# Causal mask and cumulated forget logarithms of the attention: from float32 matmuls to single-pass (float32r) matmuls, the logarithms as high and low parts

## The reference

```python
s = einsum('bqhd,bkhd->bhqk', q[:, q0:q1], k[:, :q1]) * scale
if cum is not None:
    s = s + (cq - ck)                 # cum = cumsum(log_sigmoid(f_logit + b))
s = where((k_pos <= q_pos) & key_valid, s, NEG_INF)
p = softmax(s); out = einsum('bhqk,bkhd->bqhd', p, v[:, :q1])
...
o_mla = block_causal_attention(q, k, v, 96 ** -0.5, key_valid)          # 8 heads
o_fox = block_causal_attention(fq, fk, fv, 64 ** -0.5, key_valid, cum)  # 8 heads
```

## Time and profile before

| | us |
|---|---|
| median of 3 runs | 1728.81 |
| those runs | 1722.48 to 1732.06 |
| profiled execution, its own time | 1722.41 |
| its span, first to last instruction | 1720.6 |
| PE busy (89% of the span) | 1523.9 |
| DVE busy (60%) | 1026.8 |
| MLA half of the attention, about | 342 to 370.5 |
| fox half of the attention, about | 370.5 to 415 |
| output projection, about | 415 to 445 |

### The profile page before, as it was taken

One profiled execution on the slowest core, in us unless ns is written; L12 is line 12 of the kernel. 1 busy time (PEld: TensorE's weight loads), 2 busy tenths in 40 slices (PEclk: granted clock), 3 DMA queues, 4 the chain that ended last, 5 costly groups with the idle time before them and its releaser, 6 DMA issues.

```text
span 1720.6 us, 22658 instructions
## 1 busy us (share of the span) xinstructions
PE 1523.9 (89%) x8228; PEld 1161.9 (68%) x8228; DVE 1026.8 (60%) x2104; ACT 533.0 (31%) x1069; POOL 558.6 (32%) x361
## 2 busy tenths in 40 slices
PE   6999989999699999999999989878787778777876
PEld 6999988678599999998889988433333333333332
DVE  5554355655233325998984744657676766758555
ACT  4443353352244335443116421312121212121111
POOL 3555353000134432001001402454454544444540
PEclk9999999899799998999999999898999998899998
DMA  6666699819979997998975836799999999999994
GB/s 264 241 227 247 245 350 378 279 46 342 386 284 371 370 366 284 365 371 308 346 255 196 342 105 275 307 428 426 428 426 427 427 427 427 426 427 427 427 427 194
DMA packets 98724, 571.87 MB, mean 332 GB/s; under 512 B 10960, under 2 KB 11088, under 8 KB 48976
## 3 DMA queue, kind: packets, MB, share of 16 engines
q1 hardware_dynamic: 60624, 297.89, 47.3%
q0 software_dynamic: 36864, 268.45, 37.1%
q10 hardware_dynamic: 1152, 4.43, 0.7%
HBM read 569.68 MB, written 135.27 MB: 410 GB/s over the span
## 4 chain that ended last, share of the span: by engine, by line
PE 67%; DMA 20%; DVE 8%; issue 2%; ACT 2%; SPq 2%; POOL 0%; ACTq 0%; DVEq 0%; POOLq 0%
DMA arena<-pairs,eidx 16%; PE ps L2125 11%; PE ps L1612 9%; PE ps L1614 9%; PE ps L1613 9%; PE ps L1957 5%; PE ps L2090 3%; PE ps L1663 2%; PE ps L1665 2%; PE ps L1664 2%; DMA ring<-pairs,eidx 2%; PE ps L1974 2%; DVE arena L1530 2%; DMA ring<-in_stream 1%; PE ps L1627 1%
## 5 line engine op out<-in xcount | busy, mean ns | idle before, releaser
L2125 PE MATMUL ps<-arena 128*128 128x512 f32 x720 | 346.3, 636 | 85.3 <-ACT arena L997 85.2
L634 POOL TENSOR_TENSOR w_lo<-ring,w_hi 128x1024 fp32r<-128x1024 f32 x82 | 216.2, 2638 | 446.7 <-DVE w_lo L1059 366.3
L2125 PEld LDWEIGHTS ps<-arena 128*128 128x128 f32 x720 | 144.2, 204 | 285.5 <-issue 174.1
L1612 PE MATMUL ps<-u_hi,w_hi 128*128 128x256 f32 (+1 forms) x1056 | 305.1, 289 | 9.9 <-DVE u_lo L1028 9.9
L1614 PE MATMUL ps<-u_hi,w_lo 128*128 128x256 f32 (+1 forms) x1056 | 303.3, 287 | 0.0
L1613 PE MATMUL ps<-u_lo,w_hi 128*128 128x256 f32 (+1 forms) x1056 | 302.9, 287 | 0.0
L1530 DVE CUSTOM_DVE_ANT_0 arena<-arena 128x1024 f32<-128x1024 f32 x180 | 218.9, 1223 | 138.7 <-DMA arena<-pairs,eidx 138.7
L664 POOL DMA_INDIRECT arena<-pairs,eidx x180 | 213.4, 1185 | 254.8 <-PE ps L2125 202.4
L681 ACT ACTIVATE w_hi<-ring 128x1024 fp32r<-128x1024 f32 x188 | 197.9, 1056 | 191.5 <-PE ps L1665 77.5
L1612 PEld LDWEIGHTS ps<-u_hi,w_hi 128*128 128x128 f32 x1056 | 201.9, 191 | 12.6 <-issue 10.7
L1614 PEld LDWEIGHTS ps<-u_hi,w_lo 128*128 128x128 f32 x1056 | 202.2, 192 | 0.0
(11 more groups left out here) (301 smaller groups left out, 2461.0 us busy)
## 6 DMA issues: line engine op xcount, KB each, us to landing
ring<-in_stream SPq DMA_DIRECT2D x130, 1024.0 KB, 7.0
pairs<-in_peer_u SPq DMA_DIRECT2D x128, 512.0 KB, 7.6
pairs<-in_peer_v SPq DMA_DIRECT2D x128, 512.0 KB, 8.8
arena<-in_ada SPq DMA_DIRECT2D x32, 768.0 KB, 6.3
arena<-pairs,eidx POOLq DMA_INDIRECT x180, 17.9
ring<-pairs,eidx POOLq DMA_INDIRECT x76, 17.3
h<-in_x_t SPq DMA_DIRECT2D x1, 1088.0 KB, 7.8
arena<-in_keys ACTq DMA_DIRECT2D x1, 1024.0 KB, 7.0
```

The source lines that it names most:

```text
L634: pool.tensor_tensor(lo[:, half, :], ring[:, slot, e * HALF:(e + 1) * HALF], hi[:, half, :], ALU.subtract).then_inc(used if e else lo_done, 1)
L1612: pe.matmul(dst, hi[:, half, block], x[0][:, b, 0:w], start=(b == 0), stop=False)
L2125: mm = pe.matmul(ps[:, Y_BANKS[j // TOPK] + half, :], diag[:, n % DIAGS, :], slot_of(n)[:, D + half * 512:D + half * 512 + 512], start=(hd ...
```

## The change

The mask and the identity are copied once by ScalarE into float32r tables (`masking`), the column table `sel` with sign plus and minus into `signs`. VectorE makes, instead of `ncumz`, a float32r copy of `cumz` (`cum_hi`) and the remainder (`cum_lo`). TensorE adds the mask with one float32r matmul, and the logarithms with four (high and low, along queries and along keys) instead of two float32 ones; the minus sign moves into the `signs` table.

```diff
-        ncumz = view(T)
+        place(parts_end)
+        cum_hi, cum_hi_f = parts("cum_hi", 1, T)
+        cum_lo, _ = parts("cum_lo", 1, T)
+        masking, _ = parts("masking", 2, P)
+        signs, _ = parts("signs", 2, HEADS)
...
# ScalarE, between the raw queries and the raw keys
+            act.activation(masking[:, 0, :], ident, ACT.Copy).then_inc(masking_made, 1)
+            act.activation(masking[:, 1, :], C("neg_mask"), ACT.Copy).then_inc(masking_made, 1)
+            act.activation(signs[:, 0, :], C("sel"), ACT.Copy).then_inc(masking_made, 1)
+            act.activation(signs[:, 1, :], C("sel"), ACT.Copy, scale=-1.0).then_inc(masking_made, 1)
...
# VectorE, before the first maximum
-            dve.tensor_scalar(ncumz, cumz, -1.0, None, ALU.mult).then_inc(cum_done, 1)
+            dve.wait_ge(q_raw_mm, 4)
+            then(dve.tensor_copy(cum_hi[:, 0, :], cumz), cum_done)
+            dve.tensor_tensor(cum_lo[:, 0, :], cumz, cum_hi_f[:, 0, :], ALU.subtract).then_inc(cum_done, 1)
...
# TensorE, scores_of(n)
-                    pe.matmul(dst, cumz[:, X0 + t * P:X0 + (t + 1) * P], C("sel")[:, f:f + 1].broadcast_to([P, keys_n]), start=False, stop=False)
-                    pe.matmul(dst, C("sel")[:, f:f + 1].broadcast_to([P, P]), ncumz[:, 0:keys_n], start=False, stop=False)
-                pe.matmul(ps[:, n % 3, keys_n - P:keys_n], ident, C("neg_mask"), start=False, stop=True).then_inc(s_mm, 1)
+                    for cum in (cum_hi, cum_lo):
+                        pe.matmul(dst, cum[:, 0, X0 + t * P:X0 + (t + 1) * P], signs[:, 0, f:f + 1].broadcast_to([P, keys_n]),
+                                  start=False, stop=False)
+                        pe.matmul(dst, signs[:, 1, f:f + 1].broadcast_to([P, P]), cum[:, 0, 0:keys_n], start=False, stop=False)
+                if n == 0:
+                    pe.wait_ge(masking_made, 4)
+                pe.matmul(ps[:, n % 3, keys_n - P:keys_n], masking[:, 0, :], masking[:, 1, :], start=False, stop=True).then_inc(s_mm, 1)
```

More of the change, by code:

```diff
@@ L269, in program @@
         assert spot[0] <= act_end - RING * T
+        place(parts_end)
[3 more added lines that the diff above has]
+        signs, _ = parts("signs", 2, HEADS)
+        assert spot[0] <= parts_end + 2 * HEADS * QK
         place(split)
@@ L427, in program @@
         cum_done = sem("cum_done")
+        masking_made = sem("masking_made")
         kpe_done = sem("kpe_done")
@@ L1856, in scores_of @@
                     if f + t == 0:
-                        pe.wait_ge(cum_done, 3)
+                        pe.wait_ge(cum_done, 4)
                     pe.matmul(dst, fqz[:, f, q], fk[:, f // 2, 0:keys_n], start=True, stop=False)
-                    pe.matmul(dst, cumz[:, X0 + t * P:X0 + (t + 1) * P], C("sel")[:, f:f + 1].broadcast_to([P, keys_n]), start=False, stop=False)
-                    pe.matmul(dst, C("sel")[:, f:f + 1].broadcast_to([P, P]), ncumz[:, 0:keys_n], start=False, stop=False)
-                pe.matmul(ps[:, n % 3, keys_n - P:keys_n], ident, C("neg_mask"), start=False, stop=True).then_inc(s_mm, 1)
+                    for cum in (cum_hi, cum_lo):
[5 more added lines that the diff above has]
+                pe.matmul(ps[:, n % 3, keys_n - P:keys_n], masking[:, 0, :], masking[:, 1, :], start=False, stop=True).then_inc(s_mm, 1)
             def turn_probs(n):
```

## The result

| | before | changed |
|---|---|---|
| median, us | 1728.01 (8 runs, 1721.44 to 1732.06) | 1742.06 (8 runs, 1735.08 to 1745.95) |
| profiled execution, its own time | 1722.41 | 1735.38 |
| mean granted clock of that execution | 0.950 | 0.935 |

The ratio is 1.0081, 95% interval 1.0056 to 1.0106: slower by less than 1% but clear of the scatter, where 1726.9 us (range 1719.5 to 1733) and no measurable change were forecast. In a second measurement of the changed kernel it was 1.0115 [1.0051, 1.0178]. The profiled executions differ by 12.97 us.

A forecast was written before the change was run, and what follows sets the result against it. The DMA queue, not TensorE, was taken to set the second feed-forward's start. Terms -0.8 - 0.28 - 0.6 + 0.45 - 0.7 gave -1.9 us, from 1728.81 to 1726.9 us, range 1719.5 to 1733.

The forecast's parts named there:

- the clock falls: Rival: lighter streaming drops TensorE's clock in the MLA half, +3.1 us a pair, some +25 us, 1752 us; chance 0.04.
- T0: SyncE's issue at 379.92 us after the first modulation addition; savings before it count, later ones mostly lengthen TensorE's 15.58 us idle.
- Prices of the single-pass matmuls: Attention on TensorE: a float32r matmul costs 0.124 us over 272 columns, 0.11 over 144 or 128.
- Single-pass is not single-pass: Rival: broadcast operands make the float32r logarithm matmuls cost float32's price; 1738.3 us; chance 0.03.
- MLA pair: Two MLA attention units, 3.91 us: lighter odd mask saves 0.13 us per loop, about six loops, -0.8 us.
- Fox pair: Two fox attention units, 4.99 us: TensorE saves 0.70, taken as -0.6 us, one full pair before T0.
- VectorE ahead of the first maximum: Before the first softmax: copy and subtraction replace the negation, so the first maximum starts 0.45 us later.
- ScalarE's four copies: Between raw queries and raw keys: about 0.9 us, covered by ScalarE's waits for TensorE, cost 0; uncovered up to 1.5.
- After T0: Fox half: TensorE's some 3 us saved goes into idle time; earlier transfer issues bring -0.7 us.
- All savings count: Rival: every TensorE saving in the attention reaches the total, -5.1 us, 1723.7 us; chance 0.13.
- nothing arrives: Rival: the later first maximum and ScalarE's copies eat the gain, 0 to +1.5 us, about 1729.3; chance 0.15.

The follow-up runs named there:

- e5: Changed kernel plus two unused float32 matmuls of 512 columns filling TensorE's wait before the first softmax: 1728.86 us, ratio 0.9974.
- e12: Changed kernel plus two unused single-pass matmuls of 256 columns in each of units 0 to 3 only: 1726.34 us, ratio 0.9972.
- e3: Changed kernel with the mask of the 16 MLA units added in float32, fox units as changed: 1728.5 us, ratio 0.9989.
- e4: Kernel before, all attention matmuls float32, with ScalarE's copies and VectorE's high part and remainder made but not read: 1738.58 us, ratio 1.0037.
- e11: Changed kernel plus two unused single-pass matmuls of 256 columns in each of units 8 to 15 only: 1750.64 us, ratio 1.0126.
- e2: Changed kernel with the mask in float32 in all units, logarithms still as single-pass high and low parts: 1731.51 us, ratio 1.0011.
- e13: Changed kernel with only the first three masks (units 0 to 2) in float32: 1741.85 us, ratio 1.0038.
- e14: Kernel before (ScalarE's copies made) with single-pass masks in units 0 to 2 alone: 1736.76 us, ratio 1.0039.
- e8: Changed kernel with the MLA units' mask in float32 and the wait before the first softmax filled with two matmuls: 1728.26 us, ratio 0.9977.
- e9: Kernel before with its eight modulation additions behind the odd MLA units instead of in the fox half: 1728.98 us, ratio 0.9999.
- e10: Changed kernel with the wait before the first softmax filled and the modulation additions moved to the MLA half: 1720.57 us, ratio 0.9941.
- e15: Changed kernel with the wait before the first softmax filled and the modulation additions behind units 1, 4, 7 to 22: 1720.98 us, ratio 0.9924.
- e1: Kernel before with the mask in single-pass format in all 32 units, logarithms still float32 with the negation: 1749.64 us, ratio 1.0105.
- e17: e15 plus two unused single-pass products of 256 columns in the units of the heads that are not fox: 1725.15 us, ratio 0.9956.

## Why the prediction was wrong

**Where it failed.** The step that failed is the last rival, "the clock falls": the clock at 1.00 in the whole attention was taken as given, and the rival got 0.04. What it says against itself, "in an MLA pair only the masks of 0.22 change out of 3.91 us", looked at the pair in steady work. The pair alone doesn't decide (e5 and e12 hold 1.00 with light masks, e3, e4 and e11 stay at 0.50 with heavy ones or added columns). What the runs show in its place: the clock goes to 0.50 for 44 us right at the wait ahead of the pairs, which the change lengthened from 1.26 to 2.12 us. With matmuls put into that wait the loss is gone (1.0081 became 0.9974). The prediction had both terms of this wait in hand, the first maximum 0.45 us later and masks lighter by 0.11 to 0.16. It priced them as time on the path and didn't see that they lengthen an idle time of TensorE. The rival's own argument, less streamed, is not refuted: without light masks in the MLA half there is no loss (e2, e3), and the masks behind the wait have a share (e13, e14). How the loss divides between the wait and the lighter work stays open. The rival's price of +3.1 us a pair was too high too: at 1.2 GHz a pair takes 5.98 us, +2.07, since not all links of the loop are TensorE's: VectorE's maximum takes 0.44 us in both.

**T0.** Right, and it is why the clock costs anything. 44 us at 0.50 delayed T0 by 15.56 us, and 13.47 of them reached the norm. The other half of the rule, that savings after T0 go into TensorE's idle time, shows in e8, whose clock stayed at 1.00:

```profile
460.42 5.63 PE L1640 MATMUL ps<-arena,con 128*128 128x256 f32 x16 [18.96 <-ACT arena L717]
```

T0 was 379.67 there, and the norm starts as late as before (459.94) in spite of the shorter fox pairs. "Near 18" was forecast for this idle time.

Where the transfers don't wait for the attention, TensorE no longer waits for them at the norm (e9, e10, e15).

**Prices of the single-pass matmuls.** Right: 0.11 for mask and 144 columns, 0.12 for 272. "Single-pass is not single-pass" falls. The equal lengths of the weight loads, which the prediction held against 0.06 for the short ones, pointed the right way.

**MLA pair.** Forecast 3.75 to 3.80, measured 3.74 at clock 1.00 (e5), against 3.91.

**Fox pair.** Forecast 4.3 to 4.5, measured 4.26 to 4.40 against 4.99 and 5.00: -0.6 to -0.7, where -0.6 was taken.

**VectorE ahead of the first maximum.** Forecast +0.45, measured +0.48.

**ScalarE's four copies.** Nothing, as forecast: TensorE's wait of 0.53 us ahead of the first scores is the same in both kernels.

**After T0.** Forecast -0.7; not confirmed. In the profiles above T0 to landing is 74.03 us instead of 76.12, but the second profile of the changed kernel has 77.15 (395.05 to 472.20), and the kernel before with the filled wait 77.12. Two executions of one kernel differ here by 3.1 us, more than the whole term. The shares of the first two fox pairs after T0, 0.71 and 0.96, were 0.76 and 0.89.

**All savings count / nothing arrives.** Neither can be read from the changed kernel. Without the fall it would, by these terms, have come out at about the forecast, 0.9989: e5, with the wait filled, is at 0.9974 [0.9946, 1.0001].

**What stays open.** Which way an execution goes at A, and so the spread of one kernel from 1722 to 1741 us. All 12 executions of the changed kernel and all 9 of e1 took 1735 us or more, while e14, which has the same first masks as e1 and so should have the same B, has four of ten under 1733: the masks of the later units have a share, and no profile here shows how. No execution of the changed kernel was profiled in which the clock fell at A. Nor was the changed kernel's wait filled without adding work, so idle time and streamed work are not separated. Only one execution of each was profiled; that the longer ones among the others are those with the fall is inferred from their mean clocks (e13: 0.939 to 0.942 up to 1733 us, 0.925 to 0.933 above), not seen.

## What to carry to other kernels

Before shortening work on TensorE, list its idle times in the stage, not only its busy ones. Where a change lets TensorE finish earlier ahead of a wait, or makes the other engine of that wait later, ask what the clock does behind it, and whether the work that follows can bring it back. Where the clock is lost, ask what is queued behind the slowed stage: here it was a DMA queue. Taking that dependence away gained nothing alone (e9: 0.9999); together with the filled wait and the change it gave 0.6 to 0.8% over before (e10, e15). And a single profile showing 1.00 doesn't say that every execution does.

## What the runs showed of the hardware that was not expected

- TensorE stayed at 1.2 GHz for 42 us (e11: 64 us, e17: 52 us) while the profile has it busy without a gap, with 128x128 float32 transposes, weighings over 16 rows and scores. The Trainium skill, "TensorE: Matmul & The Clock Gate", Part 1, says that the default is throttled and that activity releases it. The fall behind an idle time agrees with that (0.78 from 346 to 348 us, behind the wait of 2.12); busy time as the profile counts it was not enough here for the release.
- The first fox scores stood at 383.77 us in the changed kernel and the clock was back at about 391.5 (0.62 from 390 to 392), with no idle time in between; in e17 it took from 389.91 to about 405. The same kind of work brought it back after 8 and after 15 us.
- The same kernel ran from 1721.44 to 1741.15 us, and the profiles show the clock already differing ahead of the attention: it falls or stays at the same wait of 1.07 to 1.09 us, eight times against twelve.
- A float32r matmul over 128 columns costs 0.11 us and over 272 columns 0.12: short ones don't get cheaper with their columns.
